# Upper half of y turned tile by tile inside the attention; output weight splits moved up; output products in its last four steps

## What is computed

```python
for l in range(DEPTH):                       # 2 layers
    h = rms_norm(x, norm_g[l]) * (1 + sc[:, None]) + sh[:, None]
    qa, ka, va, ga, qb, kb, vb, gb, qn, kn, vn, gn = split_proj(h @ w_in[l])
    ...
    ya = (rms_norm(oa, diff_subln[l]) * (1 - lam_init)).reshape(b, s, A_W) * jax.nn.silu(ga)
    yb = map_query_blocks(lambda q_blk: gqa_attend(q_blk, kb_all, vb_all), qb) * jax.nn.silu(gb)
    yn = neighbourhood_attend(qn, kn, vn, kn_c, vn_c, nat_rpb[l], rows) * jax.nn.silu(gn)
    y = jnp.concatenate([ya, yb, yn], axis=-1) @ w_out[l]     # the product that is moved
    ...                                      # layer 0: the same for the 256 rows of context
    x = x + gt[:, None] * y
```

## Time and profile before

| | us |
|---|---|
| median of 3 runs | 1280.89 |
| lowest, highest | 1278.64, 1281.61 |
| the profiled execution | 1277.03 |
| its span from first to last instruction | 1275.3 |
| mean granted clock of PE | 0.951 |
| PE busy | 1150.9 |
| DVE busy | 724.8 |
| ACT busy | 602.3 |
| POOL busy | 252.5 |

### The profile page before, as it was taken

The page is one execution under the profiler, slowest core; times in us unless marked ns, Lnnn a source line. Parts: engine busy times, 40 slices in busy tenths (PEclk is TensorE's granted clock), DMA queues, the critical chain, the costliest instruction groups (busy, mean ns, idle before and its releaser), DMA issues.

```text
span 1275.3 us, 16699 instructions
## 1 busy us (share of the span) xinstructions
PE 1150.9 (90%) x5877; PEld 913.7 (72%) x5877; DVE 724.8 (57%) x1322; ACT 602.3 (47%) x1174; POOL 252.5 (20%) x324
## 2 busy tenths in 40 slices
PE   5978799898988977999989898999889999999987
PEld 2666577676666765678767686877678887888875
DVE  3466776776751754654454666564465555565543
ACT  3433453434771454464564554444444445544553
POOL 1482330363004112302300203000021111121100
PEclk8988899898998999899999999998899999999999
DMA  9745354323102322122101664553446655434301
GB/s 336 137 162 177 96 144 132 117 82 117 50 32 72 112 77 92 51 82 83 67 34 66 237 218 159 162 186 126 138 151 191 186 182 152 130 117 132 117 1 50
DMA packets 79002, 157.92 MB, mean 124 GB/s; under 512 B 5761, under 2 KB 6057, under 8 KB 78665
## 3 DMA queue, kind: packets, MB, share of 16 engines
q1 hardware_dynamic: 75592, 147.41, 36.4%
q0 software_dynamic: 3328, 9.46, 3.3%
HBM read 153.73 MB, written 3.11 MB: 123 GB/s over the span
## 4 chain that ended last, share of the span: by engine, by line
PE 70%; DVE 11%; ACT 7%; POOL 5%; issue 4%; DMA 2%; SPq 0%; ACTq 0%; POOLq 0%; DVEq 0%
PE bank L707 16%; PE bank L709 16%; PE bank L708 16%; PE bank L848 5%; PE bank L823 3%; PE bank L833 3%; POOL small L1415 3%; PE bank L923 2%; DVE work L1625 2%; DVE w_lo L1605 2%; PE bank L896 2%; ACT w_hi L1019 2%; PE bank L908 1%; PE bank L727 1%; POOL stage L490 1%
## 5 line engine op out<-in xcount | busy, mean ns | idle before, releaser
L707 PE MATMUL bank<-w_lo,h_hi 128*128 128x512 f32 (+1 forms) x1152 | 464.0, 403 | 27.0 <-DVE h_lo L1674 10.8
L708 PE MATMUL bank<-w_hi,h_lo 128*128 128x512 f32 (+1 forms) x1152 | 448.7, 389 | 0.0
L709 PE MATMUL bank<-w_hi,h_hi 128*128 128x512 f32 (+1 forms) x1152 | 448.1, 389 | 0.0
L1605 DVE TENSOR_TENSOR w_lo<-raw,w_hi 128x1024 fp32r<-128x1024 f32 x224 | 285.5, 1280 | 209.7 <-ACT w_hi L1019 208.3
L1019 ACT ACTIVATE w_hi<-raw 128x1024 fp32r<-128x1024 f32 x224 | 235.9, 1057 | 312.2 <-PE bank L709 265.3
L707 PEld LDWEIGHTS bank<-w_lo,h_hi 128*128 128x128 f32 x1152 | 223.8, 194 | 79.0 <-issue 30.6
L709 PEld LDWEIGHTS bank<-w_hi,h_hi 128*128 128x128 f32 x1152 | 223.1, 194 | 45.3
L708 PEld LDWEIGHTS bank<-w_hi,h_lo 128*128 128x128 f32 x1152 | 224.0, 194 | 40.1 <-issue 0.2
L848 PE MATMUL bank<-work,stage 128*128 128x128 f32 x640 | 95.7, 293 | 1.8 <-ACT stage L1206 1.6
L848 PEld LDWEIGHTS bank<-work,stage 128*128 128x128 f32 x640 | 86.2, 207 | 3.4 <-ACT stage L1206 2.8
L1206 ACT ACTIVATE stage<-bank 128x512 f32<-128x512 f32 (+1 forms) x96 | 50.3, 524 | 74.6 <-PE bank L833 74.4
(11 more groups left out here) (172 smaller groups left out, 1095.1 us busy)
## 6 DMA issues: line engine op xcount, KB each, us to landing
raw<-in_b_w_in_dram SPq DMA_DIRECT2D x80, 512.0 KB, 3.6
raw<-in_w_in_dram SPq DMA_DIRECT2D x56, 512.0 KB, 3.7
raw<-in_a_w_in_dram SPq DMA_DIRECT2D x48, 512.0 KB, 4.3
raw<-in_w_ada_dram SPq DMA_DIRECT2D x32, 512.0 KB, 3.6
work<-in_w_ada_dram SPq DMA_DIRECT2D x16, 512.0 KB, 11.4
raw<-in_w_out_dram SPq DMA_DIRECT2D x16, 512.0 KB, 3.5
raw<-in_a_w_out_dram SPq DMA_DIRECT2D x16, 512.0 KB, 3.5
raw<-in_b_w_out_dram SPq DMA_DIRECT2D x8, 512.0 KB, 3.5
```

The lines of the kernel that those rows point to most:

```text
L707: pe.matmul(bank, hT(h_hi, ph, kt, tt), w_lo[:, s, k, lo:lo + w], start=first, stop=False)
L708: pe.matmul(bank, hT(h_lo, ph, kt, tt), w_hi[:, s, k, lo:lo + w], start=False, stop=False)
L709: mm = pe.matmul(bank, hT(h_hi, ph, kt, tt), w_hi[:, s, k, lo:lo + w], start=False, stop=last)
L1605: dve.tensor_tensor(w_lo[:, i % SPLIT, :, :], raw[:, PIECE_AT[p] % RAW, :, :], w_hi[:, i % SPLIT, :, :].bitcast(F32), ALU.subtract).then_i ...
```

## The change

Three things, in both layers of the first block:

1. The upper half of y of a tile is turned inside the attention, four steps after its last unit of kind C: tiles 0, 1, 2 of layer 0 in steps 49, 55, 61, tile 0 of layer 1 in step 29. Only the last tile's upper half is turned after the last step.
2. The splits of the first output chunk stand in steps 45, 47, 49, 51 of layer 0. In layer 1 their entries move too, and still do nothing.
3. The products of chunk 0 for tiles 0 and 1 of layer 0 stand in steps 62 to 65, two pieces (12 matmuls) behind each step's attention work; for tile 0 of layer 1 in steps 31 to 33 (6, 12 and 6 matmuls). After the last turn PE makes the remaining tiles of chunk 0, then `project` starts at chunk 1.

```diff
@@ fill_of
     for i, tt in enumerate(tts):
-        tasks.setdefault(first + i, []).append(("y", tt))
+        tasks.setdefault(first + i, []).append(("y", tt, 0))
+        done = units.index((layer, tt, "C", C_HEADS - 1)) + 4
+        if tt != tts[-1]:
+            tasks.setdefault(done, []).append(("y", tt, 1))
     for i in range(SPLIT):
-        tasks.setdefault(len(units_of(layer)) - SPLIT + i, []).append(("split", i))
+        tasks.setdefault(first + 1 + (2 if layer == 0 else 1) * i, []).append(("split", i))
     return tasks
+def output_beside(layer):
+    p = pieces_of(f"out{layer}")[:4]
+    n = len(units_of(layer))
+    if layer == 0:
+        return {n - 2: [(0, p[0]), (0, p[1])], n - 1: [(0, p[2]), (0, p[3])], n: [(1, p[0]), (1, p[1])], n + 1: [(1, p[2]), (1, p[3])]}
+    return {n - 1: [(0, p[0])], n: [(0, p[1]), (0, p[2])], n + 1: [(0, p[3])]}
@@ PE
+            def output_products(layer, work):
+                for tt, p in work:
+                    if tt == 0:
+                        weights(p)
+                    for k in range(2):
+                        product(f"out{layer}", 0, p, k, tt)
@@ PE, the step
-                            y_turn(f"out{layer}", gate, task[1], 0)
+                            if task[2] == 1:
+                                pe.wait_ge(*y_made.seen((layer, task[1], "C", C_HEADS - 1)))
+                            y_turn(f"out{layer}", gate, *task[1:])
+                    output_products(layer, output_beside(layer).get(i, ()))
@@ PE, after the last step
-                for u in units_of(layer)[-2:]:
-                    pe.wait_ge(*y_made.seen(u))
-                for tt in tiles_of(ph):
-                    y_turn(ph, gate, tt, 1)
-                project(ph)
+                tts = tiles_of(ph)
+                pe.wait_ge(*y_made.seen(units_of(layer)[-1]))
+                y_turn(ph, gate, tts[-1], 1)
+                for tt in tts[-2 if layer == 0 else -1:]:
+                    output_products(layer, [(tt, p) for p in pieces_of(ph)[:4]])
+                project(ph, chunk0=1)
@@ ACT and DVE, after the last step
-                for tt in tiles_of(ph):
-                    y_part(ph, tt, 1)
+                y_part(ph, tiles_of(ph)[-1], 1)
```

More of the change, by code:

```diff
@@ L186, in fill_of @@
             tasks.setdefault(first + i, []).append(("ada", "ada1", j))
+    units = units_of(layer)
     first = 44 if layer == 0 else 23
@@ L728, in head_turn, with project @@
                 mm.then_inc(*tpose.at(("heads", ph, c, tt)))
-            def project(ph, between=None, after_piece=None):
+            def project(ph, between=None, after_piece=None, chunk0=0):
                 tts = tiles_of(ph)
                 pairs = PROJ[ph][1] // 2
-                for c in range(PROJ[ph][0]):
+                for c in range(chunk0, PROJ[ph][0]):
                     pieces = [(ph, c, pair) for pair in range(pairs)]
@@ L865, in step @@
                         if task[0] == "y":
-                            if task[1] == 0:
+                            if task[1:] == (0, 0):
                                 for qt in (ALL_TILES if layer == 0 else X_TILES):
@@ L1230, in step @@
                         if task[0] == "y":
-                            y_part(f"out{layer}", task[1], 0)
+                            y_part(f"out{layer}", *task[1:])
                         if task[0] == "split":
@@ L1966, in _ @@
             project_with("in0", process_in, attention1(0))
-            for tt in ALL_TILES:
-                y_part("out0", tt, 1)
+            y_part("out0", ALL_TILES[-1], 1)
             project("out0", process_out)
@@ L1971, in _ @@
             project_with("in1", process_in, attention1(1))
-            for tt in X_TILES:
-                y_part("out1", tt, 1)
+            y_part("out1", X_TILES[-1], 1)
             project("out1", process_out)
```

## The result

The kernel after takes 1267.31 us in the median of four runs (1265.86 to 1270.21), beside 1281.19 for four runs of the kernel before. The ratio is 0.9907, with a 95% interval of 0.9887 to 0.9928: 11.9 us faster (9.2 to 14.5). I had forecast 1277.1, a gain of 3.8 us. The sign was right; the size was wrong by a factor of three, outside the range. The profiled execution of after took 1265.86 us, of which the span is 1264.1.

The account below looks back on a forecast made before the run. PE carries 70% of the chain, so time is won where it waits or runs at low clock. Layer 0 -3.8, collision +1.0, layer 1 -1.0: -3.8 us from 1280.89 gives 1277.1 us, forecast's own range 1274.5 to 1279.5.

Parts of the forecast that it names:

- 14.0 - 10.2 = 3.8 us gained: Layer 0: 14.0 us won at the attention's end, less 10.2 given back by turns and splits in earlier steps.
- the two terms behind it: Behind layer 0's sum: 1.0 us lost where POOL's mask meets DVE's splits, 1.0 us gained in layer 1.
- End of layer 0: From step 61's scores to tile 2's products: start moves from 405.21 to 391.2, 14.0 us gained.
- Turns in 49 and 55: Upper-half turns moved into these layer 0 steps cost 2.0 us each, 4.0 for both; bounds 0.6 and 2.5 per turn.
- Splits in 45 to 51: Layer 0's four moved splits cost 6.2 us: 2.05 in step 51, 1.4 in each of the other three.
- Collision of POOL and DVE: POOL's mask meets DVE's chunk 1 splits behind tile 2's first product: 1.0 us lost, bounds 0 and 3.5.
- Layer 1: Upper turn in step 29 and products inside: tile 1 starts at 684.9 instead of 685.9, gain 1.0 us, bounds -1 and 2.
- the low clock in the middle: Rival: stalls in steps 45 to 51 lower PE's clock over seven steps, costing 6 us, so 1283.2; chance 0.12.
- the forecast's own signs of being wrong: PE waits in the last four steps, turn plus split cost full sum or almost nothing, or clock falls in 45 to 51.
- The moved splits are hidden: Rival: splits behind turns cost 0.5 us, the lone one 1.5; 3.7 us less given back, so 1273.4; chance 0.15.
- what I said the profile would show: Steps 62 to 65: PE idle at most 0.5 us; clock 1.00 from 380 to 400; step 49 exponentials over 5 us apart.
- Tile 2's start: Tile 2's first output product of layer 0 was to start about 3.8 us earlier than 405.21.

Follow-up runs that it names:

- e3: The kernel after with splits back in steps 60 to 63 and no products inside the attention: layer 0 stretch 57.82 us, ratio to before 0.9954.
- e2: The kernel before with only the four splits of layer 0 moved, to steps 45, 47, 49, 51: layer 0 stretch 59.88 us, ratio to before 0.9981.
- e4: The kernel after with the splits of layer 0 back in steps 60 to 63, turns and products as changed: layer 0 stretch 53.51 us, ratio to before 0.9901.
- e12: The kernel after, unchanged, timed again beside the kernel before on one chip: layer 0 stretch 53.94 us, median 1266.78 us, ratio to before 0.9909.
- e9: The kernel after with the splits of layer 0 in steps 45, 47, 62, 63: layer 0 stretch 52.80 us, layer 1 stretch 26.15.
- e6: The kernel after with POOL's bias load and mask for layer 1 held behind the fourth split of chunk 1: layer 0 stretch 54.17 us, layer 1 26.14.
- e10: The kernel after with the splits of layer 0 in steps 44, 45, 46, 47: layer 0 stretch 55.28 us, layer 1 stretch 26.15.
- e13: The kernel after with splits in steps 45, 47, 62, 63 and no products inside the attention: layer 0 stretch 58.58 us, layer 1 27.84.
- e1: The kernel before, unchanged, timed and profiled again: layer 0 stretch 62.51 us, median 1279.17 us, ratio to before 1.0001.
- e11: The kernel after with upper turns one step earlier and splits in steps 45, 47, 62, 63: layer 0 stretch 51.81 us, median 1265.89 us, ratio to before 0.9901.

## Why the prediction was wrong

The mechanism was the one forecast: the turns, the splits and the products act where they were said to. What failed is the size of the terms in "14.0 - 10.2 = 3.8 us gained" and in the two terms behind it. The end of layer 0, the turns, the splits and the collision were priced too dear and layer 1's gain too low, all five in the same direction.

1. **End of layer 0: too long by 1.1 us.** From the last scores to tile 2's product I summed 17.36 us (373.84 to 391.2); the trace has 393.72 - 377.46 = 16.26. The 48 matmuls with the changes of kind took 11.3, as summed (11.4). The error is in the small pieces: transposes and values of a unit take 0.59 us from start to start (379.91 to 380.50, 383.35 to 383.94), where I had 0.72, and the last turn holds PE for 0.36 (393.36 to 393.72), where I had its duration, 0.60. A row's duration reaches into the next instruction's on PE; only the distance of starts adds up.
2. **Turns in 49 and 55: 2.0 each forecast, 1.3 and 1.5 found (e3).** I compared one interval in layer 0 with one in layer 1. A step whose neighbours are of another length can't be priced so. The trace of before already pointed to the answer: from the scores of step 43 to those of step 49 (339.85 to 357.41) it is 17.56 us for six units with four lower turns, and without a turn the next two take 3.87 (361.28 - 357.41), so a turn costs (17.56 - 3 x 3.87) / 4 = 1.5 us.
3. **Splits in 45 to 51: 6.2 forecast, 5.14 in e2, 5.04 and 4.77 in after (against e4, whose splits stand behind these scores).** Of after's 5.04, the pair of 45 and 47 has 2.7 (2.4 to 2.5 in e12 and e9) where I had 2.8, the split of 49 has 1.5 where I had 1.4, and the one of 51, which stands alone, 0.86 where I had 2.05. So the prices behind a turn were near, and nearly the whole error is the lone split, which I had read from steps 60 to 63. It is the step that makes it cheap and not that it stands alone: in e2 the split of 49 stands alone too, and costs 1.76 (5.20 us between the same two scores for 3.44 before). Why step 51 is cheaper was not tested.
4. **Collision of POOL and DVE: 1.0 forecast, 0.1 found; 0.03 by e6.** That both slow each other was right: DVE's three splits took 5.18 for 3.95 us, POOL's six mask operations 10.31 for 5.88. The rule of the Trainium skill (SBUF — State Buffer, section "Who interferes with whom") agrees with that trace. The times of the meeting were near too: the mask operations start 7.4 us behind tile 2's start and the splits 8.3, forecast as 7.5 and 8.2. The wrong step was to let any of the delay reach PE: it went into DVE's idle time ahead of the fourth split (1.98 us before, 0.77 now, see e6).
5. **Layer 1: 1.0 forecast, 1.7 found.** The pieces were priced by durations as in point 1: from the end of the upper turn to tile 1 I summed 11.35 us, and after has 10.77 from the transposes behind that turn (662.73) to 673.50. The last turn holds PE for 0.36 where I had 0.6, the last values product for 0.81 (670.87 to 671.68) where I had 0.9. e3 shows that the moved turn gives nothing here; the gain is the products'.

Points 1 to 3 are 3.4 us, 4 is 0.9 and 5 is 0.7: together the 5.0 between 3.8 and 8.8. The median of three runs from which I subtracted was too high by 1.9. The rest of the distance from 1277.1 to 1267.3, 2.9 us, is in part the execution of before that was profiled, whose layer 0 stretch was 0.5 shorter than the mean of two; some 2 us stay open, as above.

Of the rivals, the low clock in the middle came true as to its mechanism: the granted clock falls to 0.65 in steps 48 and 49. e4, with the turns but no splits there, keeps 1.00, and e2, with splits alone, falls to 0.62, so the splits bring it. It was also one of the forecast's own signs of being wrong. The price is small here: the pair of splits with the fall costs 2.4 to 2.7 us, the pair without it 2.3 to 2.4. How much of that is the clock's no run separates. Behind the fall DVE's next maximum waits 1.57 us for PE's scores (0.77 in e4), so PE is on the path there, and in e10 a fall beside the turns cost 1.6. My price, 6 us, took the low clock for seven steps; it stayed for one or two. "The moved splits are hidden" priced the four at 0.5, 0.5, 0.5 and 1.5, so 3.0 us, which is 3.2 less than 6.2 and not the 3.7 I wrote. They cost 4.8 to 5.0, so it isn't what happened either.

Most of what I said the profile would show is there: no idle time on PE over 0.5 us in steps 62 to 65, clock 1.00 from 380 to 400, exponentials 5.20 us apart in step 49, maxima about 1.1 apart, splits beside the mask at 1.7 us each. Tile 2's start missed, with 7.2 us for 3.8 behind the first turn, and so did tile 1's in layer 1, with 1.7 for 1.

## What to carry to other kernels

Sum a chain on PE by distances between starts, never by durations, and read the price of an added operation over two or more whole steps, in the stage in which it will stand. Independent matmuls put beside the last waits of a stage pay twice, for the waits and for the clock of what follows; with them in place a DVE operation can stay there cheaply: two splits cost 1.2 us beside them and 2.0 without. Where timed medians differ by less than the executions do, the same stretch in two profiles tells more than many runs.

## What the hardware showed that I had not expected

- The clock behind a stall can cost more than the stall. In e13 two splits hold PE up for 2.0 us and the lower clock behind them costs 2.8; in four other executions with a low clock at that place (before, e1, e2, e3) it costs 1.3 to 2.4.
- Exclusion between POOL and DVE is mutual and can be free: both lose (5.88 to 10.31 and 3.95 to 5.18 us), PE does not notice. With the mask behind the splits (e6) POOL still needs 8.16 us for its six, beside DVE's additions of x and stage, of which the first takes 1.10 us and those behind it about 0.8, for 0.69 in before.
- One program's executions differ by place: the first turn of layer 0 starts between 337.6 and 344.2 us, and from the next projection's first turn to layer 1's the profiles of before and after have 224.7 to 226.5 us, that of e11 220.5. From 100 to 120 us into that stretch e11 has a granted clock of 1.00; all other kernels here have 0.73 to 0.92 in windows of 10 us. I did not find what decides it.
